# One projection group list split by halves of K, beside the modulation that it needs

## The reference

```python
def first_block(x, c, rel_bias, w_ada, b_ada, norm_mix_g, w_in, ...):
    c_act = jax.nn.silu(c)
    for l in range(DEPTH):                       # DEPTH = 1
        mod = c_act @ w_ada[l] + b_ada[l]        # 2048 x 12288
        sh1, sc1, g1, sh2, sc2, g2 = [m[:, None, :] for m in jnp.split(mod, N_MOD, axis=-1)]
        h = rms_norm(x, norm_mix_g[l]) * (1.0 + sc1) + sh1
        proj = h @ w_in[l]
        u, q, k, v, ga, gb = jnp.split(proj, split_at, axis=-1)
        y_ssm = s5_branch(u, ...)                # u: 1024 columns, then a scan over time
        ...
```

## Time and profile before

| | |
|---|---|
| runs: median, lowest, highest | 3495.85, 3493.39, 3503.64 us |
| profiled execution, its span | 3494.1 us |
| busy share PE / PEld / DVE / ACT / POOL | 68 / 58 / 82 / 29 / 36% |
| HBM read | 1062.80 MB, 305 GB/s over the span |

### The profile page before, as it was taken

One profiled execution on the slowest core, in us unless ns is written; L12 is line 12 of the kernel. 1 busy time (PEld: TensorE's weight loads), 2 busy tenths in 40 slices (PEclk: granted clock), 3 DMA queues, 4 the chain that ended last, 5 costly groups with the idle time before them and its releaser, 6 DMA issues.

```text
span 3494.1 us, 38094 instructions
## 1 busy us (share of the span) xinstructions
PE 2382.4 (68%) x14750; PEld 2035.6 (58%) x14750; DVE 2875.2 (82%) x3467; ACT 1009.5 (29%) x1529; POOL 1259.2 (36%) x975
## 2 busy tenths in 40 slices
PE   8869999989899999999989899300044430003444
PEld 7859999988788888888989779200011110001111
DVE  7698867867886886887777857899999999998777
ACT  1404433434644544453565545100000000000000
POOL 6351101101110110110000000468866788887663
PEclk7779999989999999999999999655567665556777
DMA  9517968868796996896454245899999999999998
GB/s 362 211 25 284 343 241 297 328 242 286 263 324 242 325 326 240 316 324 210 157 170 133 83 159 188 326 383 427 427 427 427 407 427 425 427 427 427 427 427 346
DMA packets 223692, 1069.00 MB, mean 306 GB/s; under 512 B 24344, under 2 KB 30488, under 8 KB 157592
## 3 DMA queue, kind: packets, MB, share of 16 engines
q0 software_dynamic: 119808, 704.70, 50.6%
q1 hardware_dynamic: 103704, 361.87, 29.0%
HBM read 1062.80 MB, written 3.67 MB: 305 GB/s over the span
## 4 chain that ended last, share of the span: by engine, by line
PE 52%; DVE 18%; POOL 15%; DMA 9%; issue 4%; ACT 2%; DVEq 0%; SPq 0%; ACTq 0%
PE ps L593 52%; POOL wide L1734 6%; DMA wide<-in_up,idx_t 5%; DVE acts L2611 5%; POOL wide_b L1734 4%; POOL raws L1734 3%; DMA wide_b<-in_up,idx_t 2%; DVE wide L2539 1%; POOL a_acc L1734 1%; DMA a_raws<-in_ada 1%; DVE a_raws L2468 1%; DVE a_acc L1774 1%; DMA raws<-in_up,idx_t 1%; DVE a_raws L2465 1%; ACT acts L1274 1%
## 5 line engine op out<-in xcount | busy, mean ns | idle before, releaser
L593 PE MATMUL ps<-opa_both,w_hi 128*128 128x256 f32 (+1 forms) x5024 | 1153.8, 318 | 44.1 <-DVE opa_both L1833 23.9
L1750 DVE TENSOR_TENSOR raws_r<-raws,w_hi 128x1024 fp32r<-128x1024 f32 x607 | 729.2, 1224 | 286.0 <-ACT w_hi L1213 281.8
L593 PEld LDWEIGHTS ps<-opa_both,w_hi 128*128 128x128 f32 x5024 | 832.4, 194 | 107.2 <-issue 41.3
L593 PE MATMUL ps<-opa_both,raws_r 128*128 128x256 f32 x3152 | 883.4, 284 | 0.0
L1213 ACT ACTIVATE w_hi<-raws 128x1024 fp32r<-128x1024 f32 x607 | 637.8, 1057 | 710.8 <-PE ps L593 440.8
L593 PEld LDWEIGHTS ps<-opa_both,raws_r 128*128 128x128 f32 x3152 | 609.5, 193 | 7.4
L1649 POOL DMA_DIRECT2D a_raws<-in_ada x320 | 169.2, 529 | 1183.3 <-DVE a_acc L1774 925.8
L593 PE MATMUL ps<-opb_both,w_hi 128*128 128x512 f32 (+1 forms) x1952 | 578.3, 361 | 4.8 <-DVE opb_both L2434 4.8
L593 PE MATMUL ps<-opb_both,raws_r 128*128 128x256 f32 x1616 | 442.3, 282 | 0.0
L1774 DVE SCALAR_TENSOR_TENSOR a_acc<-a_raws,csil,a_acc 128x1024 f32<-128x1024 f32 x317 | 400.9, 1297 | 15.1 <-DMA a_raws<-in_ada 15.0
L593 PEld LDWEIGHTS ps<-opb_both,w_hi 128*128 128x128 f32 x1952 | 343.4, 190 | 57.2 <-DVE opb_both L2434 5.7
(11 more groups left out here) (438 smaller groups left out, 3411.1 us busy)
## 6 DMA issues: line engine op xcount, KB each, us to landing
raws<-in_w SPq DMA_DIRECT2D x607, 512.0 KB, 4.6
a_raws<-in_ada POOLq DMA_DIRECT2D x320, 512.0 KB, 5.8
a_raws<-in_ada SPq DMA_DIRECT2D x28, 512.0 KB, 8.5
raws<-in_ada SPq DMA_DIRECT2D x24, 512.0 KB, 9.5
acts<-in_ada SPq DMA_DIRECT2D x12, 512.0 KB, 7.8
x_res<-in_xT SPq DMA_DIRECT2D x1, 2048.0 KB, 12.6
out<-x_res SPq DMA_DIRECT2D x2, 1024.0 KB, 24.2
wide<-in_up,idx_t POOLq DMA_INDIRECT x109, 25.9
```

The source lines that it names most:

```text
L593: return nc.tensor.matmul(out, lhs, rhs, start=start, stop=stop)
L1750: TT(w_lo[p % RAW].rearrange("p b n -> p (b n)"), raw[p % RAW], w_hi[p % HI][:, :, :].rearrange("p b n -> p (b n)").bitcast(F32), ALU.subt ...
```

## The change

The chunks of the modulation are taken in another order: the first 32 give shift and scale for the first 1024 features, the last 32 for the others. After the first 32, `pair_sums(0)` and `first_cols(0)` make these columns, and ACT and DVE make the first four pieces of the operand. TensorE then multiplies the first panels (first half of K) of seven of the eight groups of `u`, each in a PSUM bank of its own, and between them its share of the later chunks. Group 7, whose bank is that of the modulation, follows when the second half is in, with the second panels of all. TensorE takes 30 of the 64 chunks, where it took 21; there are 16 places for them, where there were 12. The norm's sums go to bank 4. SP loads panels 0 to 5 behind chunks 28 to 33, and panels 6 to 12 behind chunks 38, 42, ... 62.

```diff
-for _start in (PAN["u"], PAN["out"], PAN["ff"], PAN["xr"], PAN["out2"], PAN["wq"]):
+ORDER[PAN["u"]:PAN["u"] + 16] = [PAN["u"] + i for i in (0, 2, 4, 6, 8, 10, 12, 1, 3, 5, 7, 9, 11, 13, 14, 15)]
+for _start in (PAN["out"], PAN["ff"], PAN["xr"], PAN["out2"], PAN["wq"]):
+def u_panel(j, x):
+    return PAN["u"] + (7 * x + j if j < 7 else 14 + x)
-ON_PE = [q for q in range(64) if q < 4 or q % 7 in (1, 4)]
+ON_PE = [q for q in range(64) if q < 4 or (q % 4 in (1, 2) if q < 32 else q % 8 in (1, 4, 6))]
...
 def first_group(q):
-    return (q % 2, q // 2) if q < 32 else (2 + q % 2, (q - 32) // 2)
+    return q // 32 + 2 * (q % 2), q % 32 // 2
...
+        place += [wide[:, 4 + i // 2, i % 2 * PW:(i % 2 + 1) * PW] for i in range(4)]
...
# SP
             for q in range(HALVES, 64):
-                if q == 12:
+                if q == 8:
                     sp.dma_start(b_x, a["b_x"]).then_inc(S["bload"], 16)
                 load_a(q)
-                if q >= 54 and q % 2:
-                    load_first(q // 2 - 27)
-            load_first(5)
-            for j in range(16):
-                if j == 4:
-                    sp.wait_ge(S["op"], 8)
-                    sp.dma_start(c_x, a["c_x"]).then_inc(S["cx"], 16)
-                load_w(RAW + j)
+                if 28 <= q < 34:
+                    load_first(q - 28)
+                if q >= 38 and q % 4 == 2:
+                    load_w(RAW + (q - 38) // 4)
+            sp.wait_ge(S["op"], 8)
+            sp.dma_start(c_x, a["c_x"]).then_inc(S["cx"], 16)
+            for p in range(RAW + 7, RAW + 16):
+                load_w(p)
...
# TensorE
+            def u_half(j, x):
+                panel(u_panel(j, x), ps[:, j, 0:T], opa, 8 * x, x == 0, x == 1, ("op", 0, 2) if j == 0 else None)
             direct_steps(0, 8)
             norm(0)
-            direct_steps(8, 44)
-            pair_sums(0, STEPS[31][1] if 31 not in ON_PE else STEPS[30][1])
-            direct_steps(44, 64)
-            pair_sums(2, BY_DVE).then_inc(S["adaps"], 1)
+            direct_steps(8, 32)
+            pair_sums(0)
+            pe.wait_ge(S["adacol"], 1)
+            mm(ps[:, 7, 0:32], ident, stat[:, 0, :], True, False)
+            direct_steps(32, 40)
+            pe.wait_ge(S["line"], 1)
+            pe.wait_ge(S["mean"], 1)
+            for j in range(7):
+                u_half(j, 0)
+                direct_steps(40 + 4 * j, 44 + 4 * j if j < 6 else 64)
+            pair_sums(1)
...
-            linear(PAN["u"], GRP["u"], opa, 8, ready=("op", 0, 2), swapped=True, between=turn_next)
+            for j in range(8):
+                if j == 7:
+                    pe.wait_ge(S["adacol"], 2)
+                    u_half(7, 0)
+                u_half(j, 1)
+                turn_next(j)
...
# ACT
-            operand(0, modcol(0))
+            act.wait_ge(S["gn"], 1)
+            for j in range(4):
+                operand_piece(0, j, modcol(0))
+            split_to(PAN["u"] + 7 + HI)
+            act.wait_ge(S["gn"], 2)
+            for j in range(4, 8):
+                operand_piece(0, j, modcol(0))
...
# DVE
-            ada_steps(0, 16)
-            norm_rows(lambda j: ada_steps(16 + 4 * j, 20 + 4 * j))
-            ada_steps(48, 64)
-            rest_to(2)
-            ada_cols(0)
+            ada_steps(0, 14)
+            norm_rows(lambda j: ada_steps(14 + 2 * j, 16 + 2 * j))
+            ada_steps(30, 32)
+            first_cols(0)
+            for j in range(4):
+                rest_to(j + 1)
+                low_piece(0, j)
+            for n in range(7):
+                ada_steps(32 + 4 * n, 36 + 4 * n)
+                rest_to(5 + n)
+            ada_steps(60, 64)
+            first_cols(1)
+            for j in range(4, 8):
+                low_piece(0, j)
```

More of the change, by code:

```diff
@@ L246 @@
 STEPS = _steps()
-BY_DVE = 64 - len(ON_PE)
+LAST_OF = [max(n for name, n, _ in STEPS[32 * i:32 * i + 32] if name == "ada") for i in range(2)]
 def place_free(q):
@@ L487, in build @@
         land = [S[f"land{i}"] for i in range(RAW)]
-        aland = [S[f"aland{i}"] for i in range(HALVES)] + land + [S["aland4"], S["aland5"]]
+        aland = [S[f"aland{i}"] for i in range(HALVES)] + land + [S[f"aland{i}"] for i in range(4, 10)]
         bland = [S[f"bland{i}"] for i in range(HALVES)]
@@ L582, in _ @@
             for s in range(RAW):
-                sp.wait_ge(land[s], 16 * (BEFORE + (STREAM - s + RAW - 1) // RAW))
-            for s in (0, 1, 2, 3, 10, 11):
+                sp.wait_ge(land[s], 16 * (BEFORE[s] + (STREAM - s + RAW - 1) // RAW))
+            for s in (0, 1, 2, 3, 10, 11, 12, 13, 14, 15):
                 sp.wait_ge(aland[s], 16 * PLACES.count(s))
@@ L623, in _, with linear @@
             opa, opb = (opa_hi, opa_lo), (opb_hi, opb_lo)
-            def linear(p0, g0, rhs, groups=16, ready=None, beat=None, swapped=False, sums=None, between=None,
+            def linear(p0, g0, rhs, groups=16, ready=None, beat=None, swapped=False, sums=None,
                        both=None):
@@ L723, in direct_steps, with pair_sums @@
                         m.then_inc(S["adan"], 1)
-            def pair_sums(h0, steps):
-                pe.wait_ge(S["ada"], steps)
-                for h in range(h0, h0 + 2):
+            def pair_sums(pair):
+                pe.wait_ge(S["ada"], LAST_OF[pair])
+                for h in (pair, pair + 2):
                     for b in range(8):
                         m = mm(ps[:, 7, 8 * h + b:8 * h + b + 1], a_acc[:, h, b * P:(b + 1) * P], ones[:, 0:1],
-                               False, h == HALVES - 1 and b == 7)
-                return m
+                               False, h == pair + 2 and b == 7)
+                m.then_inc(S["adaps"], 1)
+            def u_half(j, x):
+                panel(u_panel(j, x), ps[:, j, 0:T], opa, 8 * x, x == 0, x == 1, ("op", 0, 2) if j == 0 else None)
             mm(ps[:, 7, 0:32], ident, stat[:, 0, :], True, False)
@@ L1209, in split_to @@
                 for p in range(split_n[0], min(limit, STREAM)):
-                    act.wait_ge(land[p % RAW], 16 * (BEFORE + p // RAW + 1))
+                    act.wait_ge(land[p % RAW], 16 * (BEFORE[p % RAW] + p // RAW + 1))
                     if p >= HI:
@@ L1215, in split_to, with take @@
                     split_n[0] = p + 1
-            def take(p0, n, dst, swapped=False, between=None):
+            def take(p0, n, dst, swapped=False):
                 for j in range(n):
@@ L1268, in operand, with operand_piece @@
             def operand(n, shift):
-                act.wait_ge(S["gn"], n + 1)
+                act.wait_ge(S["gn"], n + 2)
                 for j in range(8):
[L1272 to L1278, removed]
+                    operand_piece(n, j, shift)
+            def operand_piece(n, j, shift):
+                act.wait_ge(S["nt"], 8 * n + j + 1)
+                for k in range(2 * j, 2 * j + 2):
+                    link(nc.scalar.activation(tmp[:, k, :], tmp[:, k, :], ACT.Identity, bias=shift[:, k:k + 1],
+                                              scale=gain[:, k:k + 1]), wait=False)
+                link.wait()
+                s = slice(2 * j, 2 * j + 2)
+                nc.scalar.activation(opa_hi[:, s, :], tmp[:, s, :], ACT.Copy).then_inc(S["nh"], 1)
             def root(n, out, x):
@@ L1325, in copy_next @@
                     copy_turned(2 * j - 7)
-            take(PAN["u"], 8, lambda j: acts[:, j, :], swapped=True, between=copy_next)
+            for j in range(8):
+                split_to(u_panel(j, 1) + 1 + AHEAD)
+                act.wait_ge(S["panel"], u_panel(j, 1) + 1)
+                nc.scalar.activation(acts[:, j, :], ps[:, j, 0:T], ACT.Copy).then_inc(S["freed_a"], 1)
+                copy_next(j)
             act.wait_ge(S["k0"], 1)
@@ L1943, in _ @@
             for j in range(8):
-                rest_to(halves(PAN["u"], j, True)[1] + 1 + AHEAD)
+                rest_to(u_panel(j, 1) + 1 + AHEAD)
                 if j == 0:
```

41 lines of the change are left out of this document (21 added, 20 removed).

## The result

The changed kernel is slower. Its median is 3572.18 us (3566.67 to 3579.42, 4 runs) against 3494.62 (3490.36 to 3503.64, 4 runs): a ratio of 1.0213, with a 95% interval of 1.0196 to 1.0230. The profiled execution has a span of 3571.3 us, 77.2 above that of before.

The account below looks back on a forecast made before the run. The opening was taken as a chain of SP, DMA and TensorE or DVE; the new panel loads close a ring. Projection end 74.6 us later plus 1 for the loop gives +75.6, so 3571.5 us, range 3545 to 3589.

Parts of the forecast that it names:

- The start: TensorE's work up to the early half panels: the first begins at 93.9 us and ends at 98.8.
- The rounds: Six alternations of SP's panel wait, chunk landing, TensorE's chunk and half panel: 15.9 or 18.2 us each, 102.3 in all.
- the second rival: Chunks behind SP's panel waits land late, 2 to 2.7 us a round, up to +16 us, so 3587; 10%.
- idle microseconds: Reason given for TensorE's low clock in the rounds: waiting lowers it, so a half panel takes 4.9 us.
- The way out: From the seventh half's end at 201.1 us through last chunks and column sums to the next projection matmul at 217.8.
- Behind the operand: Projection work left after the second operand half: 31.4 us, to 249.2.
- 1 for the loop: Allowance of 1 us for the last projection loop, where DVE's three instructions outlast TensorE's one panel.
- Downstream: Scan, heads and panel stream after the projection: no slack, so the whole shift passes to the end.
- the prediction's own signs of being wrong: Chunks landing before the panel ends they wait behind, rounds under 12 us, or a later stage giving shift back.
- the clock (first): Rival: TensorE's clock stays high in the rounds, so the loss is 45 us, 3541; 12%.
- "Not slower" (third): Rival: SP's panel waits do not hold the chunks, TensorE alone sets the end at 169 us, so 3490; 6%.
- the ring: SP's panel load waits for TensorE, whose next chunk is queued behind that load; walked six times.

Follow-up runs that it names:

- e4_dense_fill: Changed kernel with sixty unused 256-column matmuls added behind each of the first six half panels; 3561.83 us.
- e2_six_halves: Changed kernel with six early first halves instead of seven, and panels 6 to 12 loaded behind all chunks; 3509.17 us.
- e6_six_less_pe: e2_six_halves with fewer chunks on TensorE (20, not 30), VectorE taking the others; 3493.34 us.
- e7_pool_later: e6_six_less_pe with GpSimd's table work waiting until the first operand is whole; 3498.58 us.
- e8_before_pool: The kernel before the change, with only GpSimd's table work made to wait until the first operand is whole; 3503.38 us.
- e5b: Changed kernel with no half panel before the whole modulation is summed, six then, panels 6 to 12 loaded behind all chunks, 20 chunks on TensorE; 3497.53 us.

## Why the prediction was right, point by point

Place, mechanism and sign were as forecast, and the sum was off by 1.6 us of the span (+77.2 against +75.6). That it came so close is luck: it is a balance of errors, and a single trace leaves some 3.5 us open.

- **The start.** TensorE began the first half panel at 95.19 (forecast 93.9); SP's first panel went out at 100.32 (99.2 with its 0.4): +1.1. In four other traces the same program was 3.5 us earlier at the first bias, so the sign of this term is open. One error there cost nothing to speak of: the operand's first half took 13.2 us (84.27, DVE's addition of the bias, to 97.44) and not 7.9, since DVE's remainders and low pieces ran beside GpSimd, up to 2.1 us each; three chunks covered most of it, and the panel took its pieces as they came.
- **The rounds.** 106.3 us, forecast 102.3: +4.0. The term that was too small is the landing: the chunk of the first round began 8.00 us after SP's issue (forecast 7.05), that of the second 6.81 (5.8), about 1 us in each of the six, 6.5 in all; the chunks and half panels behind the landings gave 2.5 back. That is the second rival's mechanism at 6.5 of its 16 us. What delays the landing was not taken apart; the first burst ran at 385 and then 418 GB/s, as two windows show:

```profile
104.00:106.00 2.00, 0.00 (x0) 0.00 (x0) 0.93 (x1) 0.00 (x0) 0.00 (x0) 0.50 0.97 385
106.00:108.00 2.00, 0.00 (x0) 0.00 (x0) 0.35 (x1) 0.00 (x0) 0.00 (x0) 0.50 1.02 418
```

This trace too passes the 358 GB/s that the Trainium skill's page "DMA: Bandwidth & Descriptors", section Specifications, gives as the limit for one core. The chunk (3.44 us from its start to the half panel's, forecast 3.57) was nearly as reckoned; the half panel was 5.35 us (111.76 to 117.11) and 4.5 (130.77 to 135.27) with its hand-over, forecast 5.3. The reason given for the low clock, idle microseconds, is not what its row shows: in the window from 39.5 us TensorE is busy throughout, on chunks alone, at 0.51, and in the changed kernel it is busy for 39.7 of the 40 us from 60 to 100 at a granted clock of 0.50.
- **The way out.** From SP's seventh panel to the first matmul of the second half 15.98 us (206.63 to 222.61), forecast 16.3: -0.3.
- **Behind the operand.** 31.5 us (222.61 to 254.09), forecast 31.4 and 1 for the loop: the 1 was not needed.
- **Downstream.** I forecast no give-back; the shift is 79.5 us at the end of the projection and 77.2 at the end of the program, so 2.3 came back, one of the prediction's own signs of being wrong, if a small one. Between 520 and 540 us of before, and in the stretch 79.5 us later in the changed kernel, TensorE is without a gap in both and the clock differs: 0.72 and 0.87, first before, then after.

```profile
520.00:540.00 20.00, 20.00 (x127) 20.00 (x128) 5.59 (x7) 3.45 (x4) 1.06 (x2) 0.72 0.32 101
```

```profile
599.50:619.50 20.00, 20.00 (x148) 20.00 (x149) 9.34 (x11) 5.85 (x7) 2.64 (x5) 0.87 0.53 181
```

By matching instructions of the two traces, the shift fell by 4.4 us between 450 and 540 us and grew again by 2.3 later. That the clock's dips carry this is read from the windows and was not tested.

Of the rivals, the clock (first) has its price from e4_dense_fill, 13.6 us at the sums for a granted clock of 0.84 over 100 to 200 us in place of 0.60, where I had 31 for a full clock in every round. "Not slower" (third) fell with SP's waits: it needed rounds under 4.6 us, and they were 16.6 to 19.3. Its condition, no panel wait ahead of chunks, was made by e2_six_halves; even then the time was 12 us above before, and not 6 below: my 169 us for the last panel was 15 too low. The trace of e2_six_halves shows where they lie: the sums began at 135.70 and not at 130, took 5.3 us and not 3.5, TensorE was idle behind them for 9.4 and not 3.5 (ACT's order, which the change itself does not have), and the rest took 33.5, with one panel more, and not 31.4. The first of these is TensorE's share: with 20 chunks there and not 30 the sums began at 123.20 (e6_six_less_pe).

## What to carry to other kernels

Before putting a load into an in-order queue, ask what it waits for, what stands behind it, and whether the one it waits for needs that: if so it is a ring, and it lasts for the round times the number of loads, whatever the engines' shares say (six rounds, 106.3 us here; cutting the ring gave 66 to 70 back). Work taken off a path is worth only what nothing else fills: six early half panels gave 3 to 6 us of their 17, since TensorE then stood idle for 9.4 us in their place. So when work moves, look at what the next engine now waits for. And a shift at the opening went through this program nearly one to one, so the end of the first stage can be read in place of the total.

## What the runs showed of the hardware

VectorE and GpSimd slow each other when both run elementwise work with two inputs in SBUF: alone a chunk's accumulation takes 1.28 us and a product of 128x512 on GpSimd 1.05 to 1.27; side by side both come every 1.9 to 2.2 us, as if they took turns. Moving GpSimd's work moved the slowness with it (e7_pool_later, e8_before_pool). VectorE's product of one tile with a column (L1807) was held too: in e2_six_halves it took 1.76 us from 95.34, where GpSimd worked until 96.55, and 0.75 from 98.40, alone. I had not reckoned with it for e5b and e6_six_less_pe.

The Trainium skill's page "SBUF — State Buffer", section "Who interferes with whom", states such a rule: a VectorE instruction with two SBUF inputs and a GpSimd instruction that reads SBUF want the same read port, and the second to come is blocked until the first is through. The traces agree that they alternate. But from start to start chunks alone come every 1.26 us (e7_pool_later, from 107.02) and products alone every 1.14 (the changed kernel, 78.12 to 84.97), so a strict turn would give 2.4 us a pair, and in e6_six_less_pe the pairs came every 2.06. So some 0.3 us of a pair ran side by side; which part does not show.

In a list of the costliest instructions such a VectorE looks busy, not held: only the mean of one, set beside the same instruction elsewhere, tells.
